# Unnormed LRU and attention halves through the output projection, each in its own banks, with attention kept channel-major

## The reference

```python
h = rms_norm(x, mix_norm_g)
xr, yg, q, k, v = split(h @ w_in)
xr = causal_depthwise_conv(xr)
y_lru = rg_lru(xr, ...) * gelu(yg)                  # (256, 512)
q, k = rms_norm(q), rms_norm(k)                     # per head, 8 heads of 64
y_attn = softmax(q @ k.T * scale - slope * dist) @ v  # causal, (256, 512)
mixed = concat([rms_norm(y_lru, lru_out_g), rms_norm(y_attn, attn_out_g)])
x = x + mixed @ w_out
hf = rms_norm(x, ffn_norm_g)
up = causal_depthwise_conv(hf @ w_up)
gate, val = split(up)
x = x + (gelu(gate) * val) @ w_down                 # d_ff 2816
```

## Time and profile before

| what | value |
|---|---|
| three executions, median | 302.09 us |
| profiled execution, its own time | 302.12 us |
| its span, first to last instruction | 300.4 us |
| PE busy | 293.8 us (98%) |
| DVE busy | 241.6 us (80%) |
| ACT busy | 201.4 us (67%) |
| POOL busy | 3.9 us (1%) |
| granted TensorE clock, mean | 0.999 |

### The profile page before, as it was taken

One profiled execution on the slowest core, in us unless ns is written; L12 is line 12 of the kernel. 1 busy time (PEld: TensorE's weight loads), 2 busy tenths in 40 slices (PEclk: granted clock), 3 DMA queues, 4 the chain that ended last, 5 costly groups with the idle time before them and its releaser, 6 DMA issues.

```text
span 300.4 us, 4975 instructions
## 1 busy us (share of the span) xinstructions
PE 293.8 (98%) x1656; PEld 255.4 (85%) x1656; DVE 241.6 (80%) x432; ACT 201.4 (67%) x371; POOL 3.9 (1%) x21
## 2 busy tenths in 40 slices
PE   8899999999999999999999999999999999999995
PEld 8688999898998888888888888888888888888884
DVE  2898497798989766999878888888888888888864
ACT  6875498998665377877666677666666666766540
POOL 4000000000000000000000000000000000000000
PEclk9999999999999999999999999999999999999999
DMA  7999942033305810466554546383654544300003
GB/s 245 429 422 422 380 151 103 39 140 140 142 0 187 309 68 2 153 242 259 226 205 146 190 149 254 140 279 140 245 173 166 194 163 180 135 0 0 0 0 140
DMA packets 7983, 52.22 MB, mean 174 GB/s; under 512 B 896, under 2 KB 896, under 8 KB 2080
## 3 DMA queue, kind: packets, MB, share of 16 engines
q1 hardware_dynamic: 7776, 51.38, 45.4%
q0 software_dynamic: 192, 0.64, 0.5%
HBM read 50.98 MB, written 1.05 MB: 173 GB/s over the span
## 4 chain that ended last, share of the span: by engine, by line
PE 91%; DVE 3%; DMA 2%; ACT 2%; issue 0%; SPq 0%; ACTq 0%
PE bank L1203 27%; PE bank L957 15%; PE bank L958 14%; PE bank L961 14%; PE bank L1207 14%; DMA raw<-in_stream_dram 2%; PE bank L1033 1%; DVE x_tok L949 1%; ACT p_T L513 1%; PE bank L1046 1%; DVE h_both L862 1%; PE bank L1152 1%; PE bank L1151 1%; PE bank L1022 1%; PE bank L1145 1%; PE bank L1053 1%
## 5 line engine op out<-in xcount | busy, mean ns | idle before, releaser
L629 DVE TENSOR_TENSOR w_lo<-raw,w_hi 128x1024 fp32r<-128x1024 f32 x93 | 110.9, 1220 | 8.1 <-ACT w_hi L336 7.4
L336 ACT ACTIVATE w_hi<-raw 128x1024 fp32r<-128x1024 f32 x87 | 89.0, 1053 | 5.8 <-PE bank L961 4.2
L1203 PE MATMUL bank<-h_both,w_hi 128*128 128x512 f32 x352 | 87.8, 391 | 0.3 <-DVE h_both L862 0.3
L1203 PEld LDWEIGHTS bank<-h_both,w_hi 128*128 128x128 f32 x352 | 64.6, 188 | 13.0 <-issue 0.5
L1207 PEld LDWEIGHTS bank<-h_both,w_lo 128*128 128x128 f32 x352 | 48.0, 190 | 3.4
L1207 PE MATMUL bank<-h_both,w_lo 128*128 128x256 f32 x352 | 49.1, 282 | 0.0
L554 ACT ACTIVATE tanh_a<-bank 128x256 f32<-128x256 f32 x44 | 16.8, 383 | 42.6 <-PE bank L1207 42.4
L957 PE MATMUL bank<-w_hi,act_hi 128*128 128x512 f32 x88 | 34.5, 392 | 0.0
L958 PE MATMUL bank<-w_lo,act_hi 128*128 128x512 f32 x88 | 34.5, 392 | 0.0
L961 PE MATMUL bank<-w_hi,act_lo 128*128 128x512 f32 x88 | 34.2, 389 | 0.0
L887 DVE TENSOR_TENSOR ygate<-bank,tanh_a 128x256 f32<-128x256 f32 x44 | 18.5, 420 | 12.6 <-ACT tanh_a L554 12.5
(11 more groups left out here) (163 smaller groups left out, 387.7 us busy)
## 6 DMA issues: line engine op xcount, KB each, us to landing
raw<-in_stream_dram SPq DMA_DIRECT2D x46, 1024.0 KB, 4.8
x_tok<-in_x_dram SPq DMA_DIRECT2D x2, 512.0 KB, 3.7
raw<-in_stream_dram SPq DMA_DIRECT2D x2, 512.0 KB, 7.5
out_dram<-x_tok SPq DMA_DIRECT2D x4, 256.0 KB, 2.1
p_T<-in_gates_dram POOLq DMA_DIRECT2D x1, 512.0 KB, 9.6
par<-in_params_dram POOLq DMA_DIRECT2D x1, 117.0 KB, 4.7
```

Of the source, the lines that this page charges most:

```text
L336: act.activation(w_hi[u % RING][:, :], raw_unit(u), ACT.Copy).then_inc(hi_done, 1)
L629: dve.tensor_tensor(w_lo[u % RING][:, :], raw_unit(u), w_hi[u % RING][:, :].bitcast(F32), ALU.subtract).then_inc(lo_done, 1)
L1203: pe.matmul(acc[:, :], whi[:, kc, :], h_both[:, kc, :, :].rearrange("p b t -> p (b t)"), start=kc == 0, stop=False)
```

## The change

Neither half of `mixed` is normed before the projection. The LRU product and the attention product go to separate banks, and each token's factor is applied when the product is added to x. The attention output is made channel-major (channels on partitions) straight from `v` as weights and the transposed probabilities as the moving operand, so that it needs no transpose of its own. For this the probabilities are divided by their row sums before `transpose_p`, with tokens still on partitions: VectorE takes the reciprocals of two heads at a time, and GpSimd does the multiplication, 16 instructions. Quoted is the core:

```diff
+            pool.wait_ge(dist_done, TT + HEADS)
+            for h in range(HEADS):
+                pool.wait_ge(row_rec_done, h // 2 + 1)
+                for m in range(TT):
+                    part = probs[h % P_SLOTS][:, KEY_AT[m]:KEY_AT[m] + KEYS[m]]
+                    pool.tensor_scalar(part, part, row_rec[:, h, m:m + 1], None, ALU.mult).then_inc(probs_scaled, 1)
...
+            def row_reciprocals(h):
+                dve.wait_ge(probs_done, TT * (h + 2))
+                dve.reciprocal(row_rec[:, h:h + 2, :], row_sum[:, h:h + 2, :]).then_inc(row_rec_done, 1)
...
             conv_rest(3)
+            row_reciprocals(0)
             los(16)
+            row_reciprocals(2)
...
             shift(7)
-            los(19, 20)
+            row_reciprocals(4)
+            los(19)
+            row_reciprocals(6)
+            los(20)
...
             def transpose_p(h):
 
-                pe.wait_ge(probs_done, TT * (h + 1))
+                pe.wait_ge(probs_scaled, TT * (h + 1))
...
+            def attend(h, m):
+
+                half, v_head = slice(HEAD_DIM * (h % 2), HEAD_DIM * (h % 2 + 1)), slice(HEAD_DIM * h, HEAD_DIM * (h + 1))
+                queries, at = slice(P * m, SEQ), KEY_AT[m] if m == 0 else 2 * P
+                return pe.matmul(a_at(h // 2)[half, queries], v_tok[:, m, v_head], p_T[:, h, at:at + SEQ - P * m],
+                                 start=m == 0 and h // 2 % 2 == 0, stop=m == TT - 1, skip_group_check=True)
...
+            def a_sums():
+                pe.wait_ge(a_chunks, 1)
+                pe.wait_ge(y_rms_done, 1)
                 for m in range(TT):
-                    ins = pe.matmul(Y_NORM[:, SEQ + P * m:SEQ + P * (m + 1)], ones[:, :], diag[:, m, :],
+                    ins = pe.matmul(A_SUM[:, m:m + 1], a_sq_sum[:, P * m:P * (m + 1)], ones[:, 0:1],
                                     start=True, stop=True)
...
             for j in range(LC):
-                if j == LC - 1:
-                    transpose_a()
+                if j == LC - 2:
+                    a_sums()
                 u = U_O + j
                 split(u)
-                for i in range(len(O_PIECES)):
-                    ins = out_piece(u, i)
+                for i in range(len(Y_PIECES)):
+                    ins = y_piece(u, i)
...
+            y_add(0)
+            y_add(1)
+            los(26)
+            y_add(2)
+            los(27)
+            y_add(3)
...
-                dve.tensor_tensor(x_tok[:, m, cols], x_tok[:, m, cols], acc, ALU.add).then_inc(x2_done, 1)
+                dve.scalar_tensor_tensor(x_tok[:, m, cols], acc, a_rstd[:, m:m + 1], x_tok[:, m, cols],
+                                         ALU.mult, ALU.add).then_inc(x2_done, 1)
```

More of the change, by code:

```diff
@@ L165, in build_layer @@
         y_rms, y_rstd = small[:, 80:82], small[:, 82:84]
[L166 removed]
+        a_rms, a_rstd = small[:, 84:86], small[:, 86:88]
         f_ss, f_sum, f_rms, f_rstd = small[:, 200:205], small[:, 94:96], small[:, 96:98], small[:, 98:100]
@@ L250, in f_at, with a_at @@
         def f_at(m, kc):
-            tile, at = (bank[4 + kc // 4], kc % 4) if m == 0 else ((bank[2], bank[4], bank[5], bank[6])[kc % 4], kc // 4)
+            tile, at = (bank[kc // 4], kc % 4) if m == 0 else (bank[2 + kc % 4], kc // 4)
             return tile[:, P * at:P * (at + 1)]
+        def a_at(c):
+            return A_ACC[c // 2][:, SEQ * (c % 2):SEQ * (c % 2 + 1)]
         def slope(h):
@@ L482, in _, with y_to_hi, v_out @@
             p_out(7)
[L483 to L486, removed]
+            def y_to_hi(c):
+                act.activation(mix_hi[:, c, :], ygate[:, c, :], ACT.Copy,
+                               scale=par[:, LRU_G + c:LRU_G + c + 1]).then_inc(y_hi, 1)
+            def v_out(m):
                 if m == 0:
@@ L516, in f_norm @@
             def f_norm(m):
-                last = (1, len(O_PIECES) - 1)[m]
+                last = (1, len(A_PIECES) - 1)[m]
                 act.wait_ge(f_added, (1, 3)[m])
@@ L785, in _, with y_to_lo, chunk_sums @@
             los(21)
-            dve.wait_ge(y_sq, 1)
-            dve.tensor_reduce(y_sq_sum, xc[:, :, :].rearrange("p c t -> p t c"), AX_X, ALU.add).then_inc(y_chunks, 1)
+            def y_to_lo(c):
+                dve.wait_ge(y_hi, c + 1)
+                dve.scalar_tensor_tensor(mix_lo[:, c, :], ygate[:, c, :], par[:, LRU_G + c:LRU_G + c + 1],
+                                         mix_hi[:, c, :].bitcast(F32), ALU.mult, ALU.subtract).then_inc(mix_ready, 1)
+            def chunk_sums(pairs, sums, sq, done):
+                link(dve.tensor_tensor(pairs, sq[:, 0:512], sq[:, 512:1024], ALU.add))
+                dve.tensor_tensor(sums, pairs[:, 0:SEQ], pairs[:, SEQ:2 * SEQ], ALU.add).then_inc(done, 1)
@@ L788, in _ @@
+            dve.wait_ge(y_sq_done, 1)
+            chunk_sums(y_pairs, y_sq_sum, y_sq, y_chunks)
+            y_to_lo(0)
+            y_to_lo(1)
             los(22)
-            dve.wait_ge(consts, 2)
+            y_to_lo(2)
+            y_to_lo(3)
+            los(23)
             dve.wait_ge(y_rms_done, 1)
[L792 to L820, removed]
-            los(24, 25)
[L822 to L828, removed]
@@ L829, in _ @@
-            los(26, 27)
+            dve.reciprocal(y_rstd, y_rms).then_inc(y_rec, 1)
+            dve.wait_ge(a_sq_done, 2)
+            chunk_sums(a_pairs, a_sq_sum, a_sq, a_chunks)
+            for c in range(LC):
+                dve.wait_ge(a_hi, 2 if c < 2 else LC)
+                dve.scalar_tensor_tensor(mix_lo[:, LC + c, :], a_at(c), par[:, ATTN_G + c:ATTN_G + c + 1],
+                                         mix_hi[:, LC + c, :].bitcast(F32), ALU.mult, ALU.subtract).then_inc(mix_ready, 1)
@@ new lines, in _, with y_add @@
+            los(24, 25)
+            dve.wait_ge(a_rms_done, 1)
+            dve.reciprocal(a_rstd, a_rms).then_inc(a_rec, 1)
+            dve.wait_ge(y_rec, 1)
+            dve.wait_ge(a_rec, 1)
+            def y_add(i):
+                m, cols, acc = Y_PIECES[i]
+                if i == len(Y_PIECES) - 1:
+                    dve.wait_ge(unit_used, U_O + LC)
+                else:
+                    dve.wait_ge(wy_done, i + 1)
+                dve.scalar_tensor_tensor(x_tok[:, m, cols], acc, y_rstd[:, m:m + 1], x_tok[:, m, cols],
+                                         ALU.mult, ALU.add).then_inc(y_added, 1)
@@ L1001, in down_like, with warm_up @@
                              first, last, lo_ready)
-            def warm_up(products):
+            def warm_up(products, tile):
                 for _ in range(products):
-                    pe.matmul(bank[0][:, 0:P], ones[:, :], ones[:, :], start=True, stop=True)
+                    pe.matmul(tile[:, 0:P], ones[:, :], ones[:, :], start=True, stop=True)
             pe.wait_ge(ones_done, 1)
-            warm_up(WARM_UP)
+            warm_up(WARM_UP, bank[0])
             pe.wait_ge(consts, 2)
@@ L1144, in _ @@
             for h in range(HEADS):
-                pe.matmul(O_BANK[0][:, head(h)], p_T[:, h, 0:P], v_tok[:, 0, head(h)], start=True, stop=True)
+                attend(h, 0)
             pe.wait_ge(v_ready, TT)
```

123 lines of the change are left out of this document (61 added, 62 removed).

## The result

The changed kernel takes 306.56 us, the median of four executions (305.73 to 308.88), against 302.24 for the kernel before (301.57 to 302.82): a ratio of 1.0164, 95% interval 1.013 to 1.0198. It is slower by 4.3 us, where 2.3 us more were forecast. The profiled execution is the fastest of the four, 305.73 us with a span of 304.0. The other three have spans of 304.7, 305.0 and 307.1 us at a mean granted clock of 0.989, 0.989 and 0.983, where the profiled one has 0.994.

The account below looks back on a forecast made before the run. TensorE's own instructions, busy 98% of the span, were taken to set the time. Span 300.4 - 2.8 gained + 5.2 stall = 302.8, plus 1.7 around it: 304.5 us, range 299.8 to 306.8.

Parts of the forecast that it names:

- the chosen case: GpSimd and VectorE take turns, attention products overlap: 304.5 us, chance 0.42, own range 303.3 to 305.8.
- the sentence on the pause: A TensorE pause of some 5 us in two parts could also lower its clock; unpriced, on the slow side.
- attention products that do not overlap: Attention output, rival with turns: halves of the columns do not overlap, +4.9, 307.0 us, chance 0.15.
- What leaves TensorE's list: TensorE's removed, added and cheaper products: 0.87 + 2.27 - 0.3 = 2.8 us gained without the scaling.
- side-by-side choice: Attention output: even and odd heads use different column halves and overlap, 2.98 us instead of 5.56, a gain of 2.27.
- The first addition late: End of the stage: VectorE's additions and splits make `f_add(0)` and the transposes behind it about 0.3 us late.
- The stall: TensorE waits at `transpose_p` for scaled probabilities, heads 4 and 5 tight: 5.2 us with turns.
- the small steps at 52 to 57 us: GpSimd's blocks between VectorE's small steps make ScalarE's decays and exponentials up to 0.9 us late; half taken.
- The turns: GpSimd and VectorE alternate at the memory both read near 67 to 72 us; unit 16 starts at 72.4, stall 4.7 us.
- A free GpSimd: Rival: GpSimd works freely beside VectorE, attention halves overlap; stall 1.2 us, 300.5 us, chance 0.32.

Follow-up runs that it names:

- the other order of heads: Changed kernel with the attention products in head order 0, 2, 4, 6, 1, 3, 5, 7 instead of 0 to 7: 307.62 us, one execution, time not compared.
- the moved splits: Kernel with all heads scaled by VectorE, plus the splits of units 26 and 27 put before the LRU half's four additions: 298.99 us, ratio 0.9907.
- the spare products: Changed kernel with 9 spare products before the transposes of head 4 and 7 before those of head 5: 304.21 us, ratio 1.0084.

## Why the prediction was wrong

The direction, the place and the chosen case were right; the size was not. The forecast was +2.3 us and the measured difference of the medians is +4.3. The step that failed is the sentence on the pause: a lower clock of TensorE was named and put on the slow side of the forecast, but not priced, so the sum has nothing for it. It cost 1.48 us in the profiled execution and about 2.3 at the median. Two other errors, in the length of GpSimd's blocks and in the time for which it is held, cancelled. That the stated range reaches up to 306.8, just over the measured time, is luck too: that end stood for attention products that do not overlap, and the chosen case's own range ended at 305.8.

- **What leaves TensorE's list.** Forecast 2.8 us net; without the scaling the kernel gained 2.65 us. In the profiled execution, the attention output and the spread product gave 2.73 us for 0.50 + 2.27, and the two added products cost 0.36 for 0.42. The side-by-side choice was right (1.88 + 1.03 us for the eight and eight products), shown by the other order of heads. The page TensorEngine Tiling (Array Packing) of the Trainium skill, section Key Properties, says that different tiles work in parallel. The rows agree for the 128x64 shape: 8 x 0.43 = 3.44 us of streaming took 1.88.
- **The first addition late.** Forecast 0.3 us, measured 0.66 (0.85 for 0.19 before). The place and the cause were right, as the moved splits show. The scalar_tensor_tensor form, which I priced like the old one, takes 0.70 us on the path for 0.68, and GpSimd has no part in it. VectorE's row of four additions and four splits took the forecast 7.3 us (98.87 to 106.18) without an idle moment. Too long was the other side, 7.0 us for TensorE's 30 matmuls: they start 0.227 us apart there and not 0.234, which makes 6.8 (98.58 to 105.38). The rest of the 0.36 us is not accounted for one by one.
- **The stall.** Forecast 5.2 us, of which 4.7 for heads 4 and 5 and 0.5 for the small steps at 52 to 57 us. Measured 4.69 us, and nothing from the small steps: the exponential of head 4 starts at 58.08 us, where it started at 58.07. So the 0.5 us for them was put in for nothing. The 4.7 came out by luck, by two errors that cancelled: 5.5 us from the reciprocal to head 5 were forecast as 1.4 of blocks and 4.1 of turns, and 5.36 were measured as 3.04 and 2.3. I had GpSimd's block at 0.29 and 0.40 us, from an instruction of another kind; alone it is 0.60 and 0.92. And I had the two engines take turns, while in the rows only GpSimd is held: VectorE's CAST and TENSOR_TENSOR start when their semaphores allow, one even under a running block (67.17, inside the block that runs from 66.65 to 67.60), and the largest delay is the CAST's 0.18 us.
- **The turns.** The page SBUF — State Buffer of the Trainium skill, section Who interferes with whom, says that the two exclude each other for a whole instruction and that the first to issue wins. The rows agree for GpSimd's side (1.99 for 0.92 us) and not for VectorE's: its TENSOR_TENSOR starts at 67.17, while GpSimd's block from 66.65 is still running, and takes 1.27 us for 1.23.
- **The clock.** With pauses of 2.33 and 1.83 us it was at 0.50 for about 3.4 us, and unit 16 took 1.48 us more. In the median execution the whole of it is 2.2 to 2.35 us, by the spare products. The terms of the sum then read 304.5 + 2.35 - 0.5 for the smaller stall + 0.36 for the later addition = 306.7; that 306.56 was measured is not a second proof, since the 2.35 is taken from it.
- **The rivals.** A free GpSimd was the fast one. Even with no hold at all the four blocks take 3.04 us, so head 5 would be ready at 69.7 and the stall near 2.4 us, just under the 2.8 from which it decides. That rival's price was too low, but its threshold holds at full clock: the kernel with earlier reciprocals loses 2.8 us and is then as fast as the kernel before (0.36% slower with all its executions), and the one with heads 4 to 7 on VectorE is 0.7% faster. No run let GpSimd work unheld with the rest of the change as it was; holding VectorE only moved the wait.

What stays open is why the slow stretch is longer in some executions than in others, and in which executions it lies at the transposes at all, since only the profiled ones can be read. In the kernel with even and odd heads apart the clock was 0.50 from 71 to 77 us with the same two pauses (2.32 and 1.83 us), so it had fallen before the second one ended; in the changed kernel's profile it was 1.00 until 72 us and 0.50 for some 3.4 us.

## What to carry to other kernels

Work that is given to an idle engine has to be placed by when its result is needed, and priced beside what its neighbour runs at that moment: here two heads took 5.4 us on an otherwise idle GpSimd, and 1.0 us on a VectorE that looked full. When TensorE sets the time by itself, price a pause at its length and, separately, a slow clock behind it, and look at what a moved wait meets next before moving it.

## What the runs showed of the hardware

GpSimd's TENSOR_SCALAR with a column of factors takes 0.60 us for 128x128 and 0.92 us for 128x256 floats, about twice an AFFINE_SELECT of that size; beside VectorE's CASTs and TENSOR_TENSORs the larger takes up to 1.99 us, and 2.70 us (73.37 to 76.07) under a row of them in the kernel with VectorE held. VectorE is slowed by some 0.2 us at most (a CAST 0.87 for 0.69, a scan 0.89 for 0.67). Products with 64 columns of weights overlap their neighbours in the other half (1.88 us for 3.44 us of streaming), and keep part of that (2.79 us) when the neighbour in the list is in the same half. Pauses of 2.33 and 1.83 us with the transposes of one head between them came with 3.4 us at the lower clock in one execution and over 6 in another, pauses of 1.18 and 1.87 us near the start of a third with about as much as the first; a single one of 2.14 us did not, in the profiled execution.
